# The loop over the first block's two layers is written out on all five engines

## The reference

```python
for i in range(DEPTH):                                   # DEPTH = 2
    h = rms_norm(x, norm_mix_pre[i])
    z = h @ w_in[i]                                      # small parts and three gates
    c_q, c_kv, k_rope, q_c, k_c, v_c, g_a, g_b, g_c = jnp.split(z, split_points, axis=-1)
    o_a = mla_attention(c_q, c_kv, k_rope, ...)          # 8 heads
    o_b = fourier_mix(h)
    o_c = windowed_gqa(q_c, k_c, v_c, ...)               # 8 heads, 2 of keys
    merged = sigmoid(g_a) * (o_a @ w_branch_a[i]) + ...b... + ...c...
    x = x + rms_norm(merged @ w_out[i], norm_mix_post[i])
    h = rms_norm(x, norm_ffn_pre[i])
    ff = (silu(h @ w_ffn_gate[i]) * (h @ w_ffn_up[i])) @ w_ffn_down[i]   # width 2816
    x = x + rms_norm(ff, norm_ffn_post[i])
    e = (p[i] @ w_ple_proj[i]) * sigmoid(x @ w_ple_gate[i])
    x = x + rms_norm(e, norm_ple[i])
```

## Time and profile before

| | |
|---|---|
| median of three runs | 1997.49 us |
| the profiled execution, whole | 1996.03 us |
| its span, first to last instruction | 1994.3 us |
| PE busy | 1943.2 us, 97% |
| DVE, ACT, POOL busy | 1103.2, 958.8, 183.5 us |
| mean granted clock of PE | 0.997 |
| layer 0 / layer 1 of the first block | about 14 to 490 / 490 to 968 us |
| second block | about 968 us to the end |

### The profile page before, as it was taken

How to read it: one execution, slowest core, us unless ns; L and a number is a source line. 1 busy time by engine, 2 the same in 40 slices (tenths; PEclk the granted TensorE clock), 3 DMA queues, 4 the chain that set the end, 5 groups by cost and what they waited for, 6 DMA issues and landing times.

```text
span 1994.3 us, 26211 instructions
## 1 busy us (share of the span) xinstructions
PE 1943.2 (97%) x9072; PEld 1570.1 (79%) x9072; DVE 1103.2 (55%) x1330; ACT 958.8 (48%) x1256; POOL 183.5 (9%) x262
## 2 busy tenths in 40 slices
PE   8999999998999999999899999999999999999998
PEld 6777888887877888887788887688888888768886
DVE  6565664456566565445544554654465445556444
ACT  5555454435555445444544445644454444555443
POOL 4310010001321001000100022000011000100000
PEclk9999999999999999999999999999999999999999
DMA  6234555554423456555555553265555554434553
GB/s 216 94 112 148 189 192 188 189 190 150 159 64 127 175 171 223 186 185 173 175 190 189 189 180 127 87 216 184 187 181 195 189 189 169 159 105 151 187 189 105
DMA packets 204844, 332.73 MB, mean 167 GB/s; under 512 B 11344, under 2 KB 150224, under 8 KB 204752
## 3 DMA queue, kind: packets, MB, share of 16 engines
q1 hardware_dynamic: 200240, 319.33, 47.5%
q0 software_dynamic: 3120, 11.02, 1.7%
q10 hardware_dynamic: 1392, 1.21, 0.2%
HBM read 330.47 MB, written 1.05 MB: 166 GB/s over the span
## 4 chain that ended last, share of the span: by engine, by line
PE 62%; issue 31%; DVE 3%; POOL 2%; ACT 2%; DMA 1%; POOLq 0%; SPq 0%; ACTq 0%; DVEq 0%
PE ps L537 18%; PE ps L530 18%; PE ps L542 18%; PE ps L709 3%; PE ps L564 2%; PE ps L722 1%; PE ps L745 1%; PE ps L733 1%; POOL stat L2137 1%; ACT whi L1181 1%; DVE wlo L1626 1%; DMA raw<-w_in_dram 1%; POOL stat L2138 0%; DVE h L1670 0%; DVE h L1664 0%
## 5 line engine op out<-in xcount | busy, mean ns | idle before, releaser
L1626 DVE TENSOR_TENSOR wlo<-raw,whi 128x2048 fp32r<-128x2048 f32 (+1 forms) x304 | 686.2, 2257 | 536.2 <-ACT whi L1181 535.9
L1181 ACT ACTIVATE whi<-raw 128x2048 fp32r<-128x2048 f32 (+2 forms) x308 | 581.0, 1886 | 428.4 <-PE ps L542 424.2
L530 PE MATMUL ps<-whi,act_hi 128*128 128x512 f32 (+1 forms) x1632 | 446.1, 394 | 3.1 <-issue 2.2
L537 PE MATMUL ps<-wlo,act_hi 128*128 128x512 f32 (+1 forms) x1632 | 444.1, 391 | 1.6 <-DVE wlo L1626 1.6
L542 PE MATMUL ps<-whi,act_lo 128*128 128x512 f32 (+1 forms) x1632 | 437.1, 389 | 0.0
L542 PEld LDWEIGHTS ps<-whi,act_lo 128*128 128x128 f32 x1632 | 306.3, 189 | 64.2 <-DVE act_lo L1632 0.2
L537 PEld LDWEIGHTS ps<-wlo,act_hi 128*128 128x128 f32 x1632 | 304.0, 188 | 66.0 <-DVE wlo L1626 2.4
L530 PEld LDWEIGHTS ps<-whi,act_hi 128*128 128x128 f32 x1632 | 298.9, 189 | 61.5 <-issue 3.3
L1225 ACT ACTIVATE hid<-ps,stat 128x256 f32<-128x256 f32 x132 | 62.7, 475 | 284.0 <-PE ps L564 200.1
L2137 POOL TENSOR_TENSOR stat<-stat,eps 128x1 f32<-128x1 f32 x44 | 38.2, 868 | 1504.4 <-ACT prob L1212 1504.0
L530 PE MATMUL ps<-whi,hid_hi 128*128 128x512 f32 x496 | 133.2, 390 | 0.0
(11 more groups left out here) (201 smaller groups left out, 1719.4 us busy)
## 6 DMA issues: line engine op xcount, KB each, us to landing
raw<-ffn_w_gate_dram SPq DMA_DIRECT2D x88, 512.0 KB, 4.0
raw<-ffn_w_up_dram SPq DMA_DIRECT2D x88, 512.0 KB, 5.0
raw<-ffn_w_down_dram SPq DMA_DIRECT2D x88, 512.0 KB, 3.9
raw<-w_in_dram SPq DMA_DIRECT2D x64, 512.0 KB, 4.4
raw<-w_ffn_gate_dram SPq DMA_DIRECT2D x44, 512.0 KB, 4.0
raw<-w_ffn_up_dram SPq DMA_DIRECT2D x44, 512.0 KB, 5.0
raw<-w_ffn_down_dram SPq DMA_DIRECT2D x44, 512.0 KB, 4.0
raw<-a_w_qkv_dram SPq DMA_DIRECT2D x24, 512.0 KB, 4.4
```

The lines of the kernel that those rows point to most:

```text
L530: nc.tensor.matmul(o, hi, a, start=start and i == 0, stop=False)
L537: nc.tensor.matmul(o, hi, a, start=False, stop=False)
L1181: nc.scalar.activation(whi[:, u % SLOTS, 0:words], raw[:, u % SLOTS, 0:words], ACT.Copy)\
L1626: nc.vector.tensor_tensor(wlo[:, u % SLOTS, 0:words], raw[:, u % SLOTS, 0:words], whi[:, u % SLOTS, 0:words].bitcast(F32), ALU.subtract)\
```

## The change

On each of the five engines the hardware loop over the layers becomes a loop at build time: `li` is a number, and `layer1()` stands twice in the engine's program. The loops in the feed-forwards stay. Wait values and DMA addresses that were computed from the loop's register become constants. Nothing else is touched, and no line moves.

```diff
@@ -416,7 +416,7 @@
             sp.dma_start(xs[:, 0, :], A["x"][0, 0:P, :]).then_inc(s_in["x0"], 16)
-            with sp.Fori(0, DEPTH) as li:
+            for li in range(DEPTH):
                 w.layer = li
@@ -969,7 +969,7 @@
             stay_warm(WARM_START)
-            with pe.Fori(0, DEPTH) as li:
+            for li in range(DEPTH):
                 w.layer = li
                 layer1()
@@ -1478,7 +1478,7 @@
             at_start = False
-            with act.Fori(0, DEPTH) as li:
+            for li in range(DEPTH):
                 w.layer = li
@@ -2002,7 +2002,7 @@
             split(1)
-            with dve.Fori(0, DEPTH) as li:
+            for li in range(DEPTH):
                 w.layer = li
@@ -2289,7 +2289,7 @@
-            with pool.Fori(0, DEPTH) as li:
+            for li in range(DEPTH):
                 w.layer = li
                 links[0] = T
                 layer1(li)
```

## The result

The changed kernel takes 2000.91 us (median of 20 runs, 1996.58 to 2003.33), the kernel before in the same session 1997.24 us: a ratio of 1.0016 with a 95% interval of 1.0009 to 1.0023. The means are 2000.54 and 1997.27 us, so 3.3 us are to be explained; forecast were 1.1. The difference is under the 0.2% that the prediction counts as no change, but its interval lies above 1, so it is small and not nothing. One execution of the kernel before (3001.33 us) and one of a kernel further down (3773.28 us) stand far outside of the others and are left out of the means, the ratios and the latter kernel's median. It is near the fast end of a spread of nearly 7 us, so single traces are used here for places, and means of runs for totals.

A forecast was written before the change was run, and what follows sets the result against it. TensorE, busy 97% of the span, was taken to bound the kernel. Terms -0.39 + 1.68 - 0.2 gave +1.1 us on the median 1997.49, so 1998.6 us; range 1995.4 to 2001.0.

The forecast's parts named there:

- A: The forecast: TensorE's gap moves behind VectorE's chain, lower clock follows where it costs; 1998.6 us, chance 0.60.
- C: Rival: late code fetches give TensorE gaps of 2.2 us each; slower by more than 4 us, chance 0.06.
- Item 1: Between the layers, TensorE's 2.21 us jump gap goes, mostly hidden behind VectorE's chain; -0.39 us.
- Item 2: Before tile 1's turn between the layers, TensorE's gap grows to 3.54 us, lower clock behind it; +1.68 us.
- Rival B: The clock holds behind the longer gap between the layers; -0.6 us, 1996.9 us, chance 0.25.
- Items 3 and 4: The other four engines' jumps, and ScalarE's table loads at the top of the loop body: both 0 on the path.
- Item 5: Wait values in the layer bodies become constants instead of register arithmetic; -0.2 us taken, at most 7 us.
- Item 6: Second layer is read as new code, but fetches stay the same; 0, other end 2.2 us at each place.
- Item 7: The inner loops stay, and their jumps cost TensorE nothing; 0.
- D: Rival: register arithmetic was in all the short waits; faster by more than 4 us, 1991.8 us, chance 0.05.
- E: Rival: the written-out code does nothing for time, perhaps through another slow jump; 1997.5 us, chance 0.04.
- X: Theory from the experiments: lengthened small TensorE waits bring lower clock at further places, above all in attention.

The follow-up runs named there:

- the late fa_lo kernel: Kernel before, with one small VectorE memset ahead of fa_lo at two places in each layer's attention; 1999.80 us, ratio 1.0009.
- the attention-filled kernel: Changed kernel plus 8 dummy transposes ahead of TensorE's wait for fa_lo, twice in each layer's attention; 2001.88 us, ratio 1.0024.
- The repeat: The changed kernel run once more, unaltered, against the kernel before; 2000.70 us, ratio 1.0023.
- PE alone: Kernel before with only TensorE's loop over the layers written out, the other four engines keeping theirs; 1997.91 us, ratio 1.0007.
- the other four: Kernel before with SyncE, ScalarE, VectorE and GpSimd written out, TensorE keeping its loop; 1996.77 us, ratio 1.0000.

## Why the prediction came out as it did

The time, 2000.91 us, was above the 1998.6 forecast and under the 2001.0 at the end of the range. The direction and the mechanism (A) are right, the size was a third of what came. That it lies in the range is luck in part: A alone was to end at 2000.1, and the rest up to 2001.0 was meant for a gap of C that never came.

**Item 1, PE's jump: right in time, wrong in cause.** Products started 1.50 us after the turn, tile 1 at +9.38. But the 0.39 us were not the jump's; they were the lower clock in its wake, as the late fa_lo kernel showed, with the jump and without the 0.39.

**Item 2, the gap that comes instead: right, with a spread that the trace of before couldn't show.** The seam got 1.26 us longer in the profiled execution (1.29 forecast) and 1.65 us in the mean of five. The price is not a constant: in three of the five the lower level lasted about 3.4 us, in two about 6.8. Rival B, that the clock holds behind such a gap, was given 0.25. Of 13 gaps of 3.51 to 3.54 us in the traces of these kernels one was followed by full clock (the exit of the attention-filled kernel, stage 45.99). "TensorE: Matmul & The Clock Gate" of the Trainium skill, section What's actually happening, says that the point where the clock changes varies from run to run; the traces agree for gaps of 2.38 to 2.41 us, which had the lower clock behind them in 13 of 20 cases.

**Items 3 and 4, the other engines and the table loads: right as far as shown.** 1.0000 (0.9991 to 1.0009) with all four written out by themselves. On top of PE's loop written out, which is the case of the change, they came with 2.5 to 3.3 us more in the means, and which engine brings that, if any does, was not tried.

**Item 5, constants in place of register arithmetic: the step that failed, in its sign.** I took -0.2 us from a row that showed +0.1 (kT 0.9 in the layers, 1.0 in the second block) and set it aside as no difference. It was one: kT went to 1.0 in the layers as well, and its 0.226 us from copy to weight load are those of the second block. The two waits for prob rose by 0.3 us in each layer. The bodies of the two layers got 0.39 and 0.43 us longer, less 0.16 each for the earlier turn of tile 0: +0.5 where -0.2 stood.

**Item 6, code: right.** No "issue" wait came up on PE, and queue q8 moved 47 packets, 51 before. Rival C is out. **Item 7, the inner loops: right**; their rounds have the length that they had.

**Rivals D and E.** D (faster by 4 us) is out with item 5. E (nothing happens) is out: the written-out seam is another seam, and the interval of the ratio lies above 1 twice.

**The sum.** With the sizes measured, the seam 1.65 and the bodies 0.5 make 2.15 us of 3.3 (standard error of the difference about 0.5). The repeat gave 4.0, so a rest of 1.1 to 1.9 us is hardly chance alone. And the same sum would give PE alone 2.2 us, where its runs have 0.7. Most likely the rest is more time at the lower clock elsewhere: the runs of the changed kernel have a mean granted clock of 0.9947 and, again, 0.9943, those of before, of PE alone and of the other four 0.9960, 0.9959 and 0.9960. So the part that doesn't add stands in the clock too. A difference of 0.0013 of 1997 us is 2.6 us of full-clock work, by estimate one and a half stretches of 3.4 us at half clock, of which the seam has 0.4. Some of it lies where PE doesn't bound the time. Where the rest lies is open. A lower clock in attention was seen in four of 14 stages of the kernels with all five engines written out (27.75, 27.61, 27.95, 28.00, in three traces) and in none of 14 of the others, but neither test of X was a clean one. What is shown for the total is this: with the gaps at the seam and the exit covered, all of the difference is gone (1995.30 and 1995.85 us).

## What to carry to other kernels

An idle stretch of the engine that bounds the kernel has two prices, its length and the clock behind it; look where the slow products fall, ahead of a wait that hides them or behind one. Before a jump is taken out, ask what the engine waits for next: here it bought a longer wait, and 20 dummy transposes at the seam and at the exit were worth more (5.2 us) than the whole change cost (3.3 us). Put them only where every pass of the code waits. The loop could have stayed; with its gaps covered it is as fast as the straight code, in less of it.

## What the runs showed of the hardware that I had not expected

- The length of a stretch at the lower clock level varies behind one and the same gap of 3.54 us: 3.4 us in one trace and 6.8 in another, seams of 29.77 and 30.75 us. Of the 12 gaps of 3.5 us with the lower level behind them six had each length. In the six long ones it set in 0.72 to 1.59 us before PE resumed work, in the six short ones 0.63 us before or later.
- Gaps of 1.32 to 1.91 us on PE at the seam and at the exit were never followed by the lower level, unless a jump's gap of over 2 us came behind them. Pairs of waits in attention, some 0.64 + 1.02 us with four transposes of 0.63 us in all between them, sometimes were, at 1.5 to 1.7 us each (the windows at 90 us).
- A jump back over the whole layer idled PE for 2.14 to 2.40 us with 6 dummies queued ahead of it, and still for 1.75 us with 26. "Advanced Engine Details and Errata" of the Trainium skill, section Control Flow Timing, has about 108 ns for a compare-and-branch; the measurement decides, for a jump of this length.
- What stands between the last-arriving wait and the weight load counts: kT to first weight load took 0.126 us in the loop, 0.226 us with constants and that wait in front of others, and 0.052 us with constants, fewer waits and that one last.
